# Injection and output matrices of the state space turned by VectorE in 32 by 32 blocks, placed by transfers; six parameter loads moved up

## The chip, the cores and the metric

The kernel runs on one core of a Trainium2 chip. The metric is the device time of one execution, in microseconds (us); the time of a kernel is the median of several executions. In the names of the profile PE is TensorE, DVE is VectorE, ACT is ScalarE, POOL is GpSimd and SP is SyncE, which here only starts transfers.

## The reference, cut to what matters

The block has one layer: a SwiGLU feed-forward (half weight), a mixer with attention beside a state space model, and a second feed-forward. Everything is float32, with 1024 rows of 1024 features. The change touches only the matrices of the state space part:

```python
x = x + 0.5 * swiglu(rms_norm(x, ff1_norm[l]), ff1_w_gate[l], ff1_w_up[l], ff1_w_down[l])
h = rms_norm(x, mix_norm[l])
proj = h @ w_in[l]                      # q, k, v, u
...
def s5_ssm_glu(u, a_re, a_im, b_re, b_im, c_re, c_im, d_skip, log_dt, w_glu, b_glu):
    uf = u.reshape(bsz, L, N_SSM_GROUPS, SSM_GROUP_CH)          # 32 groups of 16 channels
    lam = lax.complex(a_re, a_im)                               # [32, 64]
    dt = jnp.exp(log_dt)[:, None]
    lam_bar = jnp.exp(lam * dt)
    b = lax.complex(b_re, b_im)                                 # [32, 64, 16]
    b_bar = ((lam_bar - 1.0) / lam)[..., None] * b
    c = lax.complex(c_re, c_im)                                 # [32, 16, 64]
    bu = jnp.einsum('blgh,gph->blgp', uf.astype(jnp.complex64), b_bar)
    ...                                                         # s[t] = lam_bar * s[t-1] + bu[t]
    y = jnp.real(jnp.einsum('blgp,ghp->blgh', states, c))
```

## The kernel before, in words

**Products.** Every large product is made in float32 precision from three TensorE matmuls of 128x512, on operands that are split into a high and a low part (`_hi`, `_lo`; lines 1168 to 1170). ScalarE makes the high parts, VectorE the low ones.

**First feed-forward.** Its up and gate products are 22 *instances* (`N_INST`), each made of seven block products; product (n, j) is the j-th of instance n. One block product is 12 matmuls. SP loads the weights of an instance in pairs (`load_pair`, L847 to L869, several instances before their use), ScalarE (`instance`, L1886) makes the high halves of weights, evacuates the PSUM banks (L1832) and VectorE (`instance`, L2646) makes sums, low halves and the activations. Results go to DRAM (`store_b`, `store_open`, `store_t`, L871 to L881). The down pass is 77 *steps* (7 products of 11 steps); each step needs one 256 KB `d_in` tile, loaded by `load_step` (L883 to L895) when the step `N_SLOT` = 6 places earlier is done, split by ScalarE (L1879) and VectorE (L2573). Weights `dw_*` and the residual `x` come in between, in a list written out in the SP function `ffn_loads`.

**Mixer.** After the down pass TensorE makes the columns of `proj` in the order `IN_ORDER`; the state space steps stand between them as `WITH_PE` says (a dictionary from a unit of `w_in` and half to a list): E transposes (`transposes_e`, L1481 to L1490), K products, I injections (`inject`, L1492 to L1503), Y outputs, v windows. `WITH_ACT` does the same for ScalarE. The order of the transfers is written out by hand on SP (L1083 to L1120). `store_u`, `load_u8` and `load_csn` take u through DRAM into eight-step form and bring rotation tables.

**State space.** Sequences are cut in chunks of T = 8 steps. Four kinds of matrices are needed: E (injection of u into the state at a chunk's end, 16 blocks j of 128 x 2 x 128), CL (output from the state), K (within a chunk) and rotation tables `cs`. GpSimd makes them during the first feed-forward: six small loads of `a_re`, `a_im`, `log_dt` (`small_loads`, L3082), loads of b and c, then the powers of lambda, `CT`-based output blocks, and last a loop of four rounds (`Fori`, L3328 to L3378), each of which makes four blocks j of E in `EBb`, stores them, waits for the store, makes the rotation table in the same tile and stores that:

```python
            pool.dma_start(eb_d[:, :, bass.ds(i * 4, 4), :], EBb[:, :, :, :]).then_inc(eb_stored, 16)
            pool.wait_ge(eb_stored, i * 32 + 32)
```

E comes back from DRAM in one 2 MB load (L1090) into `ebs`, with the state index on the partitions; TensorE turns it with 32 transposes of 128x128, eight calls of `transposes_e`, and ScalarE copies them into `Et` (`e_out`). The same holds for C: 4 GpSimd loads into `c_in`, 8 transposes on TensorE (`c_tiles`, before instance 10), four copies on ScalarE (`c_out`) into `CT`. VectorE's share of the parameters (`prepare`, L2706) stands before its instance 7.

Of the kernel before, what the change touches and what calls it, by code (L numbers as in the profile page):

```python
# [20 lines left out]
F32 = mybir.dt.float32  # L21
# [6 lines left out]
P = 128  # L28
# [81 lines left out]
def steps(text):  # L110
# [12 lines left out]
WITH_PE = {(1, 1): steps("m1"), (4, 0): steps("E0 E1 E2 E3"), (5, 0): steps("E4 E5 E6 E7"), (6, 0): steps("K0"), (6, 1): steps("I0"),  # L123
# [4 lines left out]
WITH_ACT = {3: steps("e0 e1 e2 e3 W3"), 4: steps("e4 e5 e6 e7 W4"), 5: steps("k0 k1 W5"), 6: steps("k2 k3"),  # L128
# [18 lines left out]

ROUND = [((kind, 2 * b + i) if kind == "K" else (kind, b), 0 if kind == "K" else i)
         for kind, b in sum((WITH_PE[o] for o in sorted(WITH_PE)), []) if kind in "KEIYv"
         for i in range(1 if kind in "Ev" else 2)]  # L150
# [266 lines left out]
def block_kernel(nc, x, ff1_norm, ff1_w_gate, ff1_w_up, ff1_w_down, mix_norm, w_in, sink, a_re, a_im,  # L417
# [85 lines left out]
    ebs = at("ebs", 64 * KB, [P, 2, NJ, P])  # L503
# [63 lines left out]
    bc_tmp = at("bc_tmp", a_v + 8 * KB, [P, 2, NJ, GH])  # L567
# [74 lines left out]
    eb_d = nc.dram_tensor("eb_scratch", (P, 2, NJ, P), F32, kind="Internal").ap()  # L642
# [72 lines left out]
    ct_ready = sem("ct_ready")  # L715
# [6 lines left out]
    pool_chain = sem("pool_chain")  # L722
    eb_stored = sem("eb_stored")
    cl_stored = [sem(f"cl_stored{i}") for i in range(2)]
# [8 lines left out]
    eb_loaded = sem("eb_loaded")  # L733
# [4 lines left out]
    e_ready = sem("e_ready")  # L738
    e_taken = sem("e_taken")
# [94 lines left out]
    def _(sp):  # L834
# [82 lines left out]

        def store_x(w, h):
            sp.dma_start(xs_d[:, :, hs(h)], xT[:, :, hs(h)]).then_inc(x_stored, 16)

        def ffn_loads(w, ends):
# [24 lines left out]
            store_b(w, N_PAIR - 1)  # L946

# [9 lines left out]
            for q in range(N_SLOT, N_DSTEP):  # L957
# [7 lines left out]
                if q in quarters:  # L965
                    load_x_back(*quarters[q])
                if q == 8:
# [73 lines left out]
        def load_csn(b):  # L1041
            sp.wait_ge(e_ready, 4 if b == 0 else 8)
# [46 lines left out]
        sp.wait_ge(eb_stored, 4 * 32 + 16)  # L1089
        sp.dma_start(ebs[:, :, :, :], eb_d).then_inc(eb_loaded, 16)  # L1090
# [74 lines left out]
    def _(pe):  # L1165
# [198 lines left out]
        def c_tiles():  # L1364

            pe.wait_ge(c_loaded, 64)
            for ri in range(2):
                for i in range(4):
                    last = nc.tensor.transpose(bank[6 + ri][:, i * P:(i + 1) * P],
                                               c_in[:, ri, i, :, :].rearrange("p a s -> p (a s)"), ident[:, :])  # L1370
                last.then_inc(ct_ready, 1)

# [52 lines left out]
        for n in range(2, N_INST):  # L1425
            if n == 10:
                c_tiles()
# [3 lines left out]
        def round_free(kind, b, i=0):  # L1431
# [13 lines left out]
            elif kind == "E":  # L1445
                pe.wait_ge(e_taken, b + 1)
# [34 lines left out]
        def transposes_e(b):  # L1481

            pe.wait_ge(eb_loaded, 16)
            round_free("E", b)
            for jj in range(2):
                for ri in range(2):
# [2003 lines left out]
```

## Time and profile before

| | us |
|---|---|
| median of 3 runs | 1592.4 (1592.19 to 1592.65) |
| span of the profiled execution | 1590.5 |
| TensorE busy in it | 1582.6 |
| VectorE, ScalarE, GpSimd busy | 1097.5, 715.6, 507.7 |
| DMA traffic | 229.01 MB, mean 144 GB/s |

The profiled execution's own span, 1590.5 us, is 1.9 us under the median of the timed runs; a time worked out from trace rows has to be raised by that to stand beside the median. TensorE was granted its full clock in all 40 slices of the page (2.4 GHz, of its two levels). The profile lists instructions with the line of the kernel that issued them. A row of a timeline gives start, duration, engine, line, operation, output<-inputs, shape, count, and in brackets the idle time before it with what ended it. For SP and for GpSimd's transfers it shows the time of the issue, not of the transfer; the views of transfers give the time from issue to landing.

### The profile page before, as it was taken

What the parts mean: (1) busy time and instruction counts of PE and PEld (TensorE: products, weight loads), DVE (VectorE), ACT (ScalarE), POOL (GpSimd) and SP (SyncE); (2) the same over time, 40 slices, a digit from 0 to 9 for tenths busy, and PEclk for the clock granted to TensorE, in tenths of its full rate; (3) what the DMA queues carried; (4) which work ended last, traced back from release to release, by engine and by line L of the source; (5) the groups of instructions that cost most, each with busy time, mean ns of one, the idle gap of its engine ahead of it and who ended that gap; (6) DMA issues with size and microseconds to landing.
All of it is one profiled execution on the core that took longest, in us unless ns stands there. A gap on an engine that the chain in (4) does not pass through costs nothing.

```text
span 1590.5 us, 22050 instructions
## 1 busy us (share of the span) xinstructions
PE 1582.6 (100%) x7553; PEld 1308.0 (82%) x7553; DVE 1097.5 (69%) x1733; ACT 715.6 (45%) x1325; POOL 507.7 (32%) x938
## 2 busy tenths in 40 slices
PE   9999999999999999999999999999999999999998
PEld 7888888888888888888887888888888888888887
DVE  7966667766678886854369768766566656578766
ACT  7544343443334445532557544434344343344444
POOL 3005788877767877323030250000000000000000
PEclk9999999999999999999999999999999999999999
DMA  8254334433488455766431141433333333885443
GB/s 285 94 80 112 118 124 146 147 135 121 167 325 260 135 139 136 268 188 147 104 133 41 51 137 53 131 108 106 106 106 107 106 106 127 310 278 152 123 110 139
DMA packets 150007, 229.01 MB, mean 144 GB/s; under 512 B 17416, under 2 KB 86672, under 8 KB 146320
## 3 DMA queue, kind: packets, MB, share of 16 engines
q1 hardware_dynamic: 146672, 219.97, 42.9%
q0 software_dynamic: 3072, 7.62, 2.5%
q8 instruction: 61, 1.00, 0.3%
q14 instruction: 42, 0.34, 0.1%
q10 hardware_dynamic: 160, 0.07, 0.0%
HBM read 153.47 MB, written 74.15 MB: 143 GB/s over the span
## 4 chain that ended last, share of the span: by engine, by line
PE 98%; POOL 1%; issue 0%; ACT 0%; DVE 0%; DMA 0%; DVEq 0%; POOLq 0%; ACTq 0%
PE bank L1168 31%; PE bank L1170 31%; PE bank L1169 31%; POOL ssq L3069 1%; PE bank L1548 1%; PE bank L1360 1%; PE bank L1575 1%; PE bank L1530 0%; PE bank L1501 0%; PE bank L1475 0%; PE bank L1561 0%; PE bank L1523 0%; PE bank L1709 0%; PE bank L1202 0%; PE bank L1395 0%
## 5 line engine op out<-in xcount | busy, mean ns | idle before, releaser
L1168 PE MATMUL bank<-hbhi,ws_lo 128*128 128x512 f32 x1040 | 405.2, 390 | 0.0
L1170 PE MATMUL bank<-hbhi,ws_hi 128*128 128x512 f32 x1040 | 404.7, 389 | 0.0
L1169 PE MATMUL bank<-hblo,ws_hi 128*128 128x512 f32 x1040 | 404.6, 389 | 0.0
L1170 PEld LDWEIGHTS bank<-hbhi,ws_hi 128*128 128x128 f32 x1040 | 195.3, 188 | 40.6
L1169 PEld LDWEIGHTS bank<-hblo,ws_hi 128*128 128x128 f32 x1040 | 195.3, 188 | 40.4
L1168 PEld LDWEIGHTS bank<-hbhi,ws_lo 128*128 128x128 f32 x1040 | 195.3, 188 | 40.4 <-issue 0.4
L1168 PE MATMUL bank<-d_hi,ws_lo 128*128 128x512 f32 x572 | 222.7, 389 | 0.0
L1170 PE MATMUL bank<-d_hi,ws_hi 128*128 128x512 f32 x572 | 222.5, 389 | 0.0
L1169 PE MATMUL bank<-d_lo,ws_hi 128*128 128x512 f32 x572 | 222.5, 389 | 0.0
L3069 POOL TENSOR_TENSOR ssq<-ssq,sqt 128x512 f32<-128x512 f32 x18 | 25.2, 1401 | 615.2 <-ACT sqt L1762 613.4
L1832 ACT ACTIVATE loc<-bank 128x512 f32<-128x512 f32 x160 | 95.6, 597 | 251.4 <-PE bank L1170 251.4
L1879 ACT ACTIVATE d_hi<-d_in 128x512 fp32r<-128x512 f32 x154 | 96.1, 629 | 201.1 <-DMA d_in<-b_scratch 200.7
L2403 DVE TENSOR_TENSOR ws_lo<-w_sum,ws_hi 128x512 fp32r<-128x512 f32 x160 | 114.7, 717 | 96.2 <-ACT ws_hi L1795 96.2
L2573 DVE TENSOR_TENSOR d_lo<-d_in,d_hi 128x512 fp32r<-128x512 f32 x154 | 112.4, 732 | 82.1 <-ACT d_hi L1879 81.9
L1795 ACT ACTIVATE ws_hi<-w_sum 128x512 fp32r<-128x512 f32 x160 | 100.2, 626 | 76.1 <-PE bank L1170 60.1
L1168 PEld LDWEIGHTS bank<-d_hi,ws_lo 128*128 128x128 f32 x572 | 107.4, 188 | 22.4
L1169 PEld LDWEIGHTS bank<-d_lo,ws_hi 128*128 128x128 f32 x572 | 107.4, 188 | 22.2
L1170 PEld LDWEIGHTS bank<-d_hi,ws_hi 128*128 128x128 f32 x572 | 107.4, 188 | 22.1
L1168 PE MATMUL bank<-hT_hi,w_lo 128*128 128x512 f32 x288 | 116.1, 403 | 0.0
L1169 PE MATMUL bank<-hT_lo,w_hi 128*128 128x512 f32 x288 | 112.4, 390 | 0.0
L1170 PE MATMUL bank<-hT_hi,w_hi 128*128 128x512 f32 x288 | 112.4, 390 | 0.0
L2403 DVE TENSOR_TENSOR ws_lo<-raw2a,ws_hi 128x512 fp32r<-128x512 f32 x78 | 55.4, 717 | 63.6 <-ACT ws_hi L1795 62.7
(322 smaller groups left out, 2700.0 us busy)
## 6 DMA issues: line engine op xcount, KB each, us to landing
b_scratch<-loc SPq DMA_DIRECT2D x42, 1024.0 KB, 7.3
d_in<-b_scratch SPq DMA_DIRECT2D x154, 256.0 KB, 3.2
raw2a<-in_ff_w_up_dram SPq DMA_DIRECT2D x42, 512.0 KB, 4.9
loc<-in_ff_w_gate_dram SPq DMA_DIRECT2D x36, 512.0 KB, 5.0
xT<-x_scratch SPq DMA_DIRECT2D x12, 1024.0 KB, 7.1
x_scratch<-xT SPq DMA_DIRECT2D x5, 2048.0 KB, 8.2
dw_lo_place<-in_ff_w_down_dram SPq DMA_DIRECT2D x8, 1024.0 KB, 7.6
x_in<-in_x_dram SPq DMA_DIRECT2D x8, 512.0 KB, 7.7
```

Source lines behind the costliest of these rows:

```text
L1168: nc.tensor.matmul(o, wl, rh, start=first, stop=False, skip_group_check=chain)
L1169: nc.tensor.matmul(o, wh, rl, start=False, stop=False, skip_group_check=chain)
L1170: return nc.tensor.matmul(o, wh, rh, start=False, stop=last, skip_group_check=chain)
L1360: last = nc.tensor.transpose(bank[X_BANK[2 * t + kh]][:, kk * P:(kk + 1) * P], x_in[t // 4][:, t % 4, k * P:(k + 1) * P], ident[:, :])
L1548: last = nc.tensor.matmul(o, qT[r, n, 2 * a:2 * a + 2, :].rearrange("p g q -> p (g q)"), kTp[r, n * CHUNK:n * CHUNK + P], start=True, stop ...
L1575: last = nc.tensor.matmul(bank[V_BANK[m]][kv * HD:(kv + 1) * HD, nn * 256:(nn + 1) * 256], vwin[:, 2 * m + nn, kv * HD:(kv + 1) * HD], pts ...
L1795: act.activation(as_block(ws_hi[b][:, :]), weights(n, s), ACT.Copy).then_inc(ws_hi_done, 1)
L1832: act.activation(snap[w][:, i, :], bank[inst_bank(n, role)][:, :], ACT.Copy).then_inc(snap_taken, 1)
L1879: act.activation(d_hi[q % N_SLOT][:, :], d_in[q % N_SLOT][:, :], ACT.Copy).then_inc(d_hi_done, 1)
L2403: dve.tensor_tensor(as_block(ws_lo[b][:, :]), weights(n, s), as_block(ws_hi[b][:, :].bitcast(F32)), ALU.subtract).then_inc(ws_lo_done, 1)
L2573: dve.tensor_tensor(d_lo[q % N_SLOT][:, :], d_in[q % N_SLOT][:, :], d_hi[q % N_SLOT][:, :].bitcast(F32), ALU.subtract).then_inc(d_lo_done, 1)
L3069: pool.tensor_tensor(ssq_of(norm, h), ssq_of(norm, h), sqt_of(norm, a), ALU.add).then_inc(ssq_done, 1)
```

## The change

- **E.** After each round's four blocks GpSimd signals `eb_made` and waits for `eb_turned` instead of for a store. VectorE turns the blocks with two block transposes, each of which transposes every 32x32 square of a 128x512 tile within its own place (`turn_e`: `EBb` to `EBt`), before its instances 15 and 20 and at the down steps 20 and 52. SP moves the squares to their places with 16 transfers per round of 32 partitions x 8 x 32 elements each (`store_et` to `et_scratch`, 256 pieces of 128 bytes a transfer): after the load of pair 18, after the last `store_b` ahead of the down pass, and at down steps 28 and 60. In the mixer SP loads the result straight into `Et` in two halves of 1 MB; the second waits for the last `hT_lo`. `load_csn(0)` and `load_csn(1)` now stand before it, the two others one place earlier than they did. `ebs`, the TensorE transposes and the ScalarE copies are gone.
- **C.** 16 SP transfers (after the load of pair 3) of 16 partitions each, then two block transposes on VectorE (`turn_c`, before instance 6) into `CT`. `prepare` goes from before instance 7 to before instance 5.
- **Parameters.** The six small loads wait for products (2,0) to (2,5) instead of (2,0), (2,3), (3,0), (3,3), (4,0) and (4,3).
- A few scratch tiles get places of their own.

The diff, cut; lines with only "..." stand for what is left out:

```diff
-WITH_PE = {(1, 1): steps("m1"), (4, 0): steps("E0 E1 E2 E3"), (5, 0): steps("E4 E5 E6 E7"), (6, 0): steps("K0"), (6, 1): steps("I0"),
+WITH_PE = {(1, 1): steps("m1"), (6, 0): steps("K0"), (6, 1): steps("I0"),
...
-WITH_ACT = {3: steps("e0 e1 e2 e3 W3"), 4: steps("e4 e5 e6 e7 W4"), 5: steps("k0 k1 W5"), 6: steps("k2 k3"),
+WITH_ACT = {3: steps("W3"), 4: steps("W4"), 5: steps("k0 k1 W5"), 6: steps("k2 k3"),
...
+E_TURN_INST = {15: 0, 20: 1}
+E_TURN_STEP = {20: 2, 52: 3}
+E_STORES = 4 * 4
...
-    c_in = at("c_in", a_v + 2 * KB, [P, 2, 4, 2, NS])
+    c_in = at("c_in", a_v + 2 * KB, [P, 2, 8, 32])
...
+    EBt = at("EBt", a_v + 6 * KB, [P, 4, 2, P])
+    ptmp_e = at("ptmp_e", a_v + 10 * KB, [P, 2, 256])
...
+        def store_et(i):
+
+            sp.wait_ge(eb_turned, 2 * i + 2)
+            for a in range(P // 32):
+                for b in range(P // 32):
+                    sp.dma_start(et_d[32 * b:32 * b + 32, 4 * i:4 * i + 4, :, 32 * a:32 * a + 32].rearrange("c j r s -> c (j r) s"),
+                                 EBt[32 * a:32 * a + 32, :, :, 32 * b:32 * b + 32].rearrange("c j r s -> c (j r) s")
+                                 ).then_inc(et_stored, 16)
+
+        def load_c():
+
+            for n, c in enumerate((c_re, c_im)):
+                for g2 in range(2):
+                    for sh in range(2):
+                        for jj in range(2):
+                            q = 64 * g2 + 32 * sh + GH * jj
+                            sp.dma_start(c_in[q:q + GH, n, :, :],
+                                         c[0].rearrange("(j a g) h s -> a g h j s", a=2, g=2)[jj, g2][:, :, 32 * sh:32 * sh + 32]
+                                         ).then_inc(c_loaded, 16)
...
                 load_pair(N_INST * w + j)
+                if (w, j) == (0, 3):
+                    load_c()
+                elif (w, j) == (0, 18):
+                    store_et(0)
...
             store_b(w, N_PAIR - 1)
+            if w == 0:
+                store_et(1)
...
+                if w == 0 and q in (28, 60):
+                    store_et(2 + (q == 60))
...
         load_in(2)
         sp.wait_ge(down_out, 28)
-        sp.wait_ge(eb_stored, 4 * 32 + 16)
-        sp.dma_start(ebs[:, :, :, :], eb_d).then_inc(eb_loaded, 16)
+        sp.wait_ge(et_stored, 4 * E_STORES * 16)
+        sp.wait_ge(eb_stored, 4 * 16 + 16)
+        sp.dma_start(Et[:, 0:8, :, :], et_d[:, 0:8, :, :]).then_inc(et_loaded, 16)
...
         load_in(3)
         sp.wait_ge(down_taken, 32)
         sp.dma_start(xs_d[:, 0:4, hs(1)], xT[:, 0:4, hs(1)]).then_inc(x_parked, 16)
+        load_csn(0)
+        load_csn(1)
+        wait_lo(sp, 2 * KD)
+        sp.wait_ge(et_loaded, 16)
+        sp.dma_start(Et[:, 8:16, :, :], et_d[:, 8:16, :, :]).then_inc(et_loaded, 16)
         load_in(4)
         store_u(0)
-        load_csn(0)
         load_u8(0)
         load_in(5)
         store_u(1)
-        load_csn(1)
+        load_csn(2)
         load_u8(1)
         store_u(2)
-        load_csn(2)
+        load_csn(3)
         load_u8(2)
-        load_csn(3)
...
         for n in range(2, N_INST):
-            if n == 10:
-                c_tiles()
             instance(n)
...
-        def transposes_e(b):
-
-            pe.wait_ge(eb_loaded, 16)
-            round_free("E", b)
-            for jj in range(2):
-                for ri in range(2):
-                    m = 2 * jj + ri
-                    last = nc.tensor.transpose(bank[round_bank("E", b)][:, m * P:(m + 1) * P],
-                                               ebs[:, ri, 2 * b + jj, :], ident[:, :])
-            last.then_inc(e_ready, 1)
-
         def inject(b):
 
-            pe.wait_ge(e_taken, 2 * b + 2)
+            pe.wait_ge(et_loaded, 16 * (b // 2 + 1))
             pe.wait_ge(u8_loaded, 16 * T * (b + 1))
...
+                if q in E_TURN_STEP and w == 0:
+                    turn_e(E_TURN_STEP[q])
...
+        def turn_e(b):
+
+            dve.wait_ge(eb_made, b + 1)
+            if b:
+                dve.wait_ge(et_stored, 16 * E_STORES * b)
+            for ri in range(2):
+                dve.transpose(EBt[:, :, ri, :], EBb[:, ri, :, :]).then_inc(eb_turned, 1)
...
-                if n == 7:
+                if n == 5:
                     prepare()
+                elif n == 6:
+                    turn_c()
+                if n in E_TURN_INST and w == 0:
+                    turn_e(E_TURN_INST[n])
                 instance(n)
...
+        def turn_c():
+
+            dve.wait_ge(c_loaded, 16 * 16)
+            for ri in range(2):
+                dve.transpose(CT[:, ri, :, :].rearrange("p j h -> p (j h)"),
+                              c_in[:, ri, :, :].rearrange("p j s -> p (j s)")).then_inc(ct_taken, 1)
...
-                    pool.wait_ge(product_done, products(2 + n, 3 * g2))
+                    pool.wait_ge(product_done, products(2, 2 * n + g2))
...
-                pool.wait_ge(product_done, products(4, 3 * g2))
+                pool.wait_ge(product_done, products(2, 4 + g2))
...
-            passed()
-            pool.dma_start(eb_d[:, :, bass.ds(i * 4, 4), :], EBb[:, :, :, :]).then_inc(eb_stored, 16)
-            pool.wait_ge(eb_stored, i * 32 + 32)
+            passed().then_inc(eb_made, 1)
+            pool.wait_ge(eb_turned, i * 2 + 2)
```

## Rows read from the trace of the kernel before

**Rows 1.** The page's head and its part 1, busy us (share) xinstructions.

```profile
span 1590.5 us, 22050 instructions
...
PE 1582.6 (100%) x7553; PEld 1308.0 (82%) x7553; DVE 1097.5 (69%) x1733; ACT 715.6 (45%) x1325; POOL 507.7 (32%) x938
```

**Rows 2.** Waits of TensorE: us in total, times, longest; the longest of four.

```profile
PE bank L1407 <- POOL eps_t L3133: 1.4, 1, 1.4
```

**Rows 3.** Chain that ended last, 650 to 700 us: start, us, group.

```profile
677.12 1.75 PE bank L1488 x16
```

**Rows 4.** Timeline of VectorE, 460 to 474 us: the split of a down step.

```profile
469.03 0.75 DVE L2573 TENSOR_TENSOR d_lo<-d_in,d_hi 128x512 fp32r<-128x512 f32 x1 [2.30 <-ACT d_hi L1879]
```

**Rows 5.** Timeline of GpSimd, 60 to 131 us.

```profile
103.34 0.82 POOL L3105 DMA_DIRECT2D par<-in_log_dt_dram  x1 [10.06 <-PE bank L1170]
111.50 0.82 POOL L3105 DMA_DIRECT2D par<-in_log_dt_dram  x1 [7.34 <-PE bank L1170]
130.16 0.82 POOL L3111 DMA_DIRECT2D b_raw<-in_b_re_dram  x1 [17.84 <-DMA par<-in_log_dt_dram]
```

**Rows 6.** Transfers, 100 to 131 us: packets, MB, share; issues with us to landing.

```profile
q0 software_dynamic: 64, 0.01, 50.9%
...
b_scratch<-loc SPq DMA_DIRECT2D x2, 1024.0 KB, 14.6
loc<-in_ff_w_gate_dram SPq DMA_DIRECT2D x2, 512.0 KB, 4.9
raw2a<-in_ff_w_up_dram SPq DMA_DIRECT2D x2, 512.0 KB, 9.1
```

**Rows 7.** Tile `eb_scratch`: ns min/median/max, first and last start in us.

```profile
L3354 POOL DMA_DIRECT2D eb_scratch<-EBb x4: 667/679/682, 339.0 to 582.5; - x4
```

**Rows 8.** Timeline of SP, 68 to 125 us (issues).

```profile
68.37 0.93 SPq L868 DMA_DIRECT2D raw2a<-in_ff_w_up_dram  x2
73.18 0.92 SPq L868 DMA_DIRECT2D loc<-in_ff_w_gate_dram  x2
```

**Rows 9.** Timeline of SP, 654 to 704 us, in the mixer.

```profile
677.77 0.34 SPq L1029 DMA_DIRECT2D u_scratch<-ust  x1
...
681.38 3.83 SPq L1039 DMA_DIRECT2D u<-u_scratch  x8
...
691.23 4.40 SPq L1039 DMA_DIRECT2D u<-u_scratch  x8
```

**Rows 10.** Timeline of ScalarE, 84 to 92 us.

```profile
84.84 0.63 ACT L1795 ACTIVATE ws_hi<-loc 128x512 fp32r<-128x512 f32 x1
86.76 0.60 ACT L1832 ACTIVATE loc<-bank 128x512 f32<-128x512 f32 x1 [1.29 <-PE bank L1170]
```

**Rows 11.** Timeline of SP, 430 to 475 us, the opening of the down pass.

```profile
445.57 0.32 SPq L873 DMA_DIRECT2D b_scratch<-loc  x1
...
457.59 3.04 SPq L895 DMA_DIRECT2D d_in<-b_scratch  x2
...
471.19 3.04 SPq L895 DMA_DIRECT2D d_in<-b_scratch  x2
```

**Rows 12.** Two windows: length, busy us of each engine, clock, DMA share, GB/s.

```profile
446.00:454.00 8.00, 8.00 (x37) 6.60 (x36) 7.96 (x10) 1.78 (x3) 6.82 (x8) 1.00 0.91 312
454.00:462.00 8.00, 8.00 (x37) 6.64 (x36) 5.96 (x10) 2.24 (x4) 0.00 (x0) 1.00 0.97 356
```

**Rows 13.** Timeline of VectorE, 655 to 760 us: the last `hT_lo`.

```profile
675.02 0.69 DVE L2368 TENSOR_TENSOR hT_lo<-htmp,hT_hi 128x512 fp32r<-128x512 f32 x1 [0.70 <-ACT hT_hi L1778]
```

**Rows 14.** Tile `u` on SP, 690 to 697 us: issues, and time to landing.

```profile
L1039 SPq DMA_DIRECT2D u<-u_scratch x8: 321/431/1198, 691.2 to 694.4; - x8
...
DMA to landing us min/median/max: 2.3/2.4/3.1
```

**Rows 15.** Timeline of TensorE, 694 to 703 us: injection 1.

```profile
701.16 1.97 PE L1501 MATMUL bank<-u,Et 128*64 128x128 f32 x32
```

**Rows 16.** The page's part 6: issues, KB each, us to landing.

```profile
k_scratch<-zero POOLq DMA_DIRECT2D x4, 56.0 KB, 3.9
```

More of the change, by code:

```diff
@@ L145 @@
 STATE_STEPS = 4 * 5 + 8
+E_TURN_INST = {15: 0, 20: 1}
+E_TURN_STEP = {20: 2, 52: 3}
+E_STORES = 4 * 4
 ROUND = [((kind, 2 * b + i) if kind == "K" else (kind, b), 0 if kind == "K" else i)
-         for kind, b in sum((WITH_PE[o] for o in sorted(WITH_PE)), []) if kind in "KEIYv"
-         for i in range(1 if kind in "Ev" else 2)]
+         for kind, b in sum((WITH_PE[o] for o in sorted(WITH_PE)), []) if kind in "KIYv"
+         for i in range(1 if kind == "v" else 2)]
 def round_number(kind, b, i=0):
@@ L722, in block_kernel @@
     pool_chain = sem("pool_chain")
+    eb_made = sem("eb_made")
+    eb_turned = sem("eb_turned")
+    et_stored = sem("et_stored")
     eb_stored = sem("eb_stored")
+    et_loaded = sem("et_loaded")
     cl_stored = [sem(f"cl_stored{i}") for i in range(2)]
@@ L1362, in x_tiles @@
                     last.then_inc(xt_done, 1)
-        def c_tiles():
-            pe.wait_ge(c_loaded, 64)
-            for ri in range(2):
[L1368 to L1371, printed above, removed]
         def first_half(norm):
@@ L1961, in ffn @@
             for n in range(N_INST * w + 2, N_INST * (w + 1)):
-                if n == 10:
-                    c_out()
                 instance(n)
@@ L1990, in x_out @@
                                ).then_inc(xt_act, 1)
-        def c_out():
-            for ri in range(2):
-                act.wait_ge(ct_ready, ri + 1)
-                for g2 in range(2):
-                    r = slice(g2 * NS, (g2 + 1) * NS)
-                    src = bank[6 + ri][r, :].rearrange("p (j g h) -> p g j h", g=2, h=GH)[:, g2]
-                    act.activation(CT[r, ri, :, :], src, ACT.Copy).then_inc(ct_taken, 1)
         act.dma_start(ident[:, :], ident_c).then_inc(ident_loaded, 16)
@@ L2058, in _ @@
             norm_hi(N_MIX, i)
-        act.wait_ge(eb_stored, 4 * 32 + 16)
+        act.wait_ge(et_stored, 4 * E_STORES * 16)
+        act.wait_ge(eb_stored, 4 * 16 + 16)
         split_in(1)
@@ L2077, in k_out @@
             act.activation(dst, src, ACT.Copy).then_inc(k_act, 1)
-        def e_out(b):
-            act.wait_ge(e_ready, b + 1)
-            if b == 0:
-                wait_lo(act, 2 * KD)
-            act.activation(Et[:, 2 * b:2 * b + 2, :, :],
-                           bank[round_bank("E", b)][:, :].rearrange("p (j r m) -> p j r m", j=2, r=2), ACT.Copy
-                           ).then_inc(e_taken, 1)
         def y_out(b):
@@ L2150, in split_later @@
             split_hi(u, free)
-        step = {"k": k_out, "e": e_out, "y": y_out, "X": exponentials, "C": p_out, "O": o_out, "g": gelu,
+        step = {"k": k_out, "y": y_out, "X": exponentials, "C": p_out, "O": o_out, "g": gelu,
                 "s": square_att, "W": split_later, "q": lambda i: act.activation(mark[:, :], eps_t[:, :], ACT.Sqrt), "n": lambda h: norm_std(N_ATT, h),
@@ L3112, in load_b @@
                            (b_re, b_im)[n][0].rearrange("(j g) p h -> g p j h", g=2)[g2]).then_inc(b_loaded, 16)
-        def load_c(n, a):
-            pool.dma_start(c_in[:, n, :, a, :], (c_re, c_im)[n][0].rearrange("(i g) h p -> (g h) i p", g=8)
-                           ).then_inc(c_loaded, 16)
         def norm(which):
@@ L3249, in _ @@
         for k in range(1, T):
-            if k % 2:
-                load_c(k // 4, k // 2 % 2)
             tt(t0, lr[k], lr[1], ALU.mult)
@@ L3345, in _ @@
                 ilink(pool.tensor_copy(cR[:, ri], rot8[:, ri, bass.ds(i * 4, 4)]))
-            q = [ptmp[:, n, 0:4 * GH].rearrange("p (j h) -> p j h", h=GH) for n in range(2)]
+            q = [ptmp_e[:, n, 0:4 * GH].rearrange("p (j h) -> p j h", h=GH) for n in range(2)]
             for t in range(T):
@@ L3359, in _ @@
             while n < NC:
-                v = [ptmp[:, m, 0:4 * n].rearrange("p (j c) -> p j c", j=4) for m in range(2)]
+                v = [ptmp_e[:, m, 0:4 * n].rearrange("p (j c) -> p j c", j=4) for m in range(2)]
                 w = [cR[:, m, :].unsqueeze(2).to_broadcast([P, 4, n]) for m in range(2)]
```

25 lines of the change are left out of this document (8 added, 17 removed).

## The prediction, made before the changed kernel ran

> **What bounds the kernel.** I read the page first: TensorE has a matmul in flight for 1582.6 of 1590.5 us [rows 1]. Then its waits: four in the whole run, none longer than the first, 1.4 us at the start [rows 2]. So from the first products to the final norm TensorE's program order is the time: whatever leaves it is gained in full, unless something becomes late enough to stop it. After that I read, stage by stage, how late the inputs of the next matmul already are: the Sync (SP) queue, ScalarE and VectorE around the places where the change puts its transfers.
>
> **What leaves TensorE.** 32 transposes of `ebs` (L1488) in two runs of 16, and 8 of `c_in` (L1369). A run of 16 takes 1.75 us [rows 3], 0.109 us each, so 40 take 4.4 us. That is the whole possible gain: the eight `e_out` and four `c_out` copies of ScalarE end no wait of TensorE, and their removal costs and brings nothing.
>
> **What is added on VectorE.** Two block transposes for C and eight for E, 512 columns each. No row shows such an operation; the nearest from below is a 512-column subtraction, 0.75 us, and twice that bounds it above [rows 4]; I take 0.75. VectorE is idle 31% of the span [rows 1] and works an instance ahead, so 1.5 us at a time (at most 3) is covered by its waits. Its new wait is for GpSimd: block 0 is turned before instance 15. GpSimd's `log_dt` issues wait for products (4,0) and (4,3), 8.16 us apart [rows 5]: 2.72 us a product, 19.04 an instance of seven. Product (4,0) is done at 103.3, so instance 4 starts near 100.6 and instance 15 eleven instances later, at about 310 to 311. Behind that wait stand the weight parts of instance 16.
>
> **The six parameter loads and GpSimd.** They now follow products (2,0) to (2,5). Products (2,4) and (2,5) are 14 x 2.72 before (4,4) and (4,5), that is at 76.1 and 78.9; the two `log_dt` loads go out there instead of at 103.3 and 111.5 [rows 5]. In the old trace GpSimd then waits until 130.16, 18.6 us after the last issue. The software queue holds 50.9% of 16 engines over 31 us with 0.01 MB [rows 6]: 15.8 us on every engine for the two, 7.9 each. Back to back behind an issue at 76.1 they land at about 95 to 103. GpSimd starts 27 to 35 us earlier, its four `c_in` issues are gone, and block 0, stored at 339.0 [rows 7], is made at about 300 to 308, before VectorE asks. Afterwards GpSimd waits for VectorE, not for a store, and a block with its table takes it about 81 us ((582.5 - 339.0) / 3 [rows 7]), against turns at instance 20 (near 406), step 20 (498) and step 52 (585): 87 us apart or more, so each block is made 6 us or more before its turn, and the last table is out near 623, long before the mixer loads it. Cost: none; were the cover gone, VectorE would wait a few us, TensorE less.
>
> **The first thing that can be late: instance 4's weights.** SP issues instance 3's second pair at 68.37 and the first of instance 4's at 73.18 [rows 8]. Between them now stand 16 `load_c` issues. Eight such issues (16 partitions) take 3.83 us [rows 9], 0.47 each, so 16 take 7.5 and instance 4's pair goes out at 76.9, just as `log_dt` reaches the engines. What that means is in the window of the old `log_dt` loads: two stores of b beside them needed 14.6 us in the median and a pair of weights 9.1, where the pair ahead of them took 4.9 [rows 6]. ScalarE takes instance 4's first block at 84.84 and must then evacuate a bank at 86.76 [rows 10]; product (3,0) is done at 103.34 - 19.04 = 84.3, so the product that needs this bank starts two products later, at 89.7, so the pair must be in SBUF by 88.3. Free: 76.9 + 5.5 = 82.4, no stall. Behind one `log_dt` load: about 78 + 9 + 3.5 = 90.5, a stall of 2.2. Behind both: near 99, 11 us. Which queue comes first is decided by some tenths of a us. I take 2.0; ends 0 and 11. The Trainium skill ("DMA: Bandwidth & Descriptors", section "Queues, rings and completion order") has each engine go round its queues a packet at a time. By that rule the pair would get its turn between the two loads, so 2.2 and not 11; the landing times above agree as far as they go.
>
> **The second: the opening of the down pass.** After the last store of b (445.57 [rows 11]) SP issues 16 `store_et` transfers, 7.5 us, while `load_step(6)` was to go one us after that store. Their 256 pieces of 128 bytes are covered by the issue if a piece costs little. The DMA engines are 0.91 busy at 446 to 454 and 0.97 at 454 to 462, 312 and 356 GB/s [rows 12]. Of the 2.5 MB of the first window 1 MB is the store ahead; 1.5 MB is pushed behind the hold, and GpSimd's 0.5 MB table, now some 12 us earlier, leaves the second: 1.0 MB at 356 GB/s, so loads land about 2.8 us later. `d_in` for step 10, issued at 457.59 or later [rows 11], is split by VectorE at 469.03 to 469.78 [rows 4], and step 10 begins at 471.19, when the load of step 15 is released [rows 11]. Slack 1.4, stall 1.4; I take 1.5. Ends: 0 (other transfers give way) and 7.5 (the hold passed on whole). `store_et(0)` at 332, `store_et(2)` at 507 and `store_et(3)` at 594 hold SP for 7.5 us too; there a load is issued 13.6 us before its step and used to land in 3 to 6, so I cost them at nothing (if their cover were gone: up to 3 us each).
>
> **The third: u8 in the mixer.** SP's list after the down pass changes: the first half of E (1 MB for 2 MB) and CL, then `load_csn(0)`, `load_csn(1)`, a wait for the last hT_lo (its subtraction starts at 675.02 [rows 13]), the second half of E (1 MB), and only then `load_in(4)` (0.5 MB), which used to be over by then. `store_u(0)` at 677.77 finds 1.5 MB ahead of it in the queue; alone it landed in 3.6 us, at 681.38 when the u8 loads begin [rows 9]. At 356 GB/s 1.5 MB take 4.4 us, 1 of them over before 677.8, so it lands 2.3 to 3.4 later, and SP passes this on: `load_u8(1)` begins at 691.23 [rows 9], its last issue, at 694.4, lands within 3.1 us, at 697.5 [rows 14], so now at about 700.2. Injection 1 was at 701.16 [rows 15]; without 32 transposes it is at 697.7. Stall 2.5; ends 0 and 3.5. K, Y and later injections keep 3 us or more.
>
> **Sum.** 1590.5 - 4.4 + 2.0 + 1.5 + 2.5 = 1592.1. The median of the runs is 1.9 above this execution's span, so 1594.0, against 1592.4. A measurement of this kernel can tell about 0.2%, 3.2 us: 1589.2 to 1595.6 is "same".
>
> **Rivals.**
> **All of it is covered (B).** For it: every term above is a race decided by 1 to 3 us, and TensorE has no wait now [rows 2]. Against: three tight places would all have to be free. 1592.4 - 4.4 = 1588.0; with one small stall of 1 us, 1589.0.
> **Small writes are slow (C), the slower side.** At 446 to 454 4096 pieces of 128 bytes go to DRAM. For it: nothing in the old trace writes pieces under 448 bytes, and the smallest pieces it reads, 4 bytes of `log_dt`, cost 7.9 us per 64 on an engine, 0.12 each. At that price, the far end, `store_et` lasts 32 us. Against: 56 KB in 448-byte pieces landed in 3.9 us [rows 16], 128 pieces, no sign of a cliff there. It decides from 0.029 us a piece (7.5 us per 256 on an engine); at 0.05, 12.8 us, the loads of steps 6 to 10 slip by 5.3 more, 1.5 becomes 6.8, and `store_et(2)` may add 2: 1599.3 to 1601. The Trainium skill (same page, "Specifications") puts 512 bytes as the least size for full rate and has a read-modify-write below it; no row here shows a 128-byte write, and the sum above goes without it.
> **Both `log_dt` loads get ahead of instance 4's pair (D).** The same race lost twice: 11 for 2.0, 1603. Against: in the old window a store of b got through beside each of the two loads, late but not stopped for both [rows 6].
> That the transposes stay on TensorE cannot be: their functions are gone.
>
> **Chances.** My case A 0.52, with 1588.5 to 1598 as its own range (0.42 of it within 0.2%, 0.10 above); B 0.28; C 0.14; D 0.06. Faster by over 0.2%: 0.28; same 0.42; slower 0.10 + 0.14 + 0.06 = 0.30. The range runs from B at its best, 1587.8, to C's middle, 1600.5, and leaves out D and C's end.
>
> **What would show it.** Right: TensorE's waits list ScalarE's bank copy or `ws` near 90 us, `d_lo` near 470, and an injection waiting for `u` near 698; GpSimd's `b_raw` load at 95 to 105; VectorE's first `EBt` at 311 to 313 with no wait for GpSimd. Wrong: no wait of TensorE between 15 and 900 us (then B); `d_in` landings over 15 us after 446 (then C); instance 4's pair landing after 95 (then D); or VectorE waiting for `EBb` at instance 15 or 20, which I cost at nothing.

## The result, and the profile after

The changed kernel takes 1614.99 us (1613.5 to 1615.99, 4 runs), the kernel before 1592.53 us beside it: a ratio of 1.014, 95% interval 1.0129 to 1.0152. It is 22.5 us slower; 1594.0 was forecast, with 1600.5 as the upper end.

The head and part 1 of the page of the changed kernel, which answer to [rows 1]:

```profile
span 1612.6 us, 22030 instructions
...
PE 1584.5 (98%) x7513; PEld 1306.6 (81%) x7513; DVE 1103.0 (68%) x1743; ACT 709.8 (44%) x1313; POOL 491.9 (31%) x930
```

TensorE has 40 instructions fewer and stands still for 28 us instead of 8. Its list of waits (us in total, times, longest us), which answers to [rows 2], says where:

```profile
PE bank L1205 <- ACT loc L1845: 13.7, 1, 13.7
PE bank L1205 <- DVE d_lo L2568: 4.7, 3, 2.4
PE bank L1514 <- issue: 1.9, 1, 1.9
PE bank L1435 <- POOL eps_t L3144: 1.4, 1, 1.4
```

The first three are the places that the prediction named: instance 4's weights (place 1, at 89 us), the opening of the down pass (place 2, 475 to 489), and injection 1 (place 3). Together they are 20.3 us. The rest shows in these windows (from and to; length, TensorE busy, granted clock, DMA share, GB/s; no other engine is listed):

```profile
100.00:104.00 4.00, 1.15 (x3) 0.50 0.60 182
104.00:108.00 4.00, 4.00 (x12) 0.55 0.01 2
108.00:112.00 4.00, 4.00 (x20) 1.00 0.00 0
```
```profile
489.00:494.00 5.00, 5.00 (x17) 0.66 1.02 410
718.00:726.00 8.00, 6.11 (x55) 0.79 0.67 212
```

After each of the three places TensorE runs for some us at the lower of its two levels (1.2 instead of 2.4 GHz). In the chain that ended last a matmul then takes 0.43 us for 0.23:

```profile
107.03 0.43 PE bank L1205
107.46 0.36 PE bank L1206
107.82 0.23 PE bank L1207
```

What that costs is the length of the stretch times (1 - clock). From the restart at 102.9 on it is 1.1 x 0.50 + 4 x 0.45 = 2.4 us at place 1; 5 x 0.34 = 1.7 at place 2; 8 x 0.21 = 1.7 at place 3, of which some 1.5 is time in which it worked. The account, by spans of the two profiled executions: -4.1 (the transposes of C 0.8, of E 3.3, from the times of the same matmul either side of the transposes) + 13.7 + 2.4 + 4.7 + 1.7 + 1.9 + 1.5 = 21.8, against 22.1 measured; the rest is in gaps too short for the list.

**Place 1.** Timelines of SP and of GpSimd, then the landing times of tile `loc` from 70 to 104 us:

```profile
68.09 0.93 SPq L874 DMA_DIRECT2D raw2a<-in_ff_w_up_dram  x2
69.06 3.85 SPq L940 DMA_DIRECT2D c_in<-in_c_re_dram  x8
72.95 4.54 SPq L940 DMA_DIRECT2D c_in<-in_c_im_dram  x8
77.53 0.98 SPq L874 DMA_DIRECT2D loc<-in_ff_w_gate_dram  x2
```
```profile
75.86 0.81 POOL L3121 DMA_DIRECT2D par<-in_log_dt_dram  x1 [1.91 <-PE bank L1207]
78.58 0.82 POOL L3121 DMA_DIRECT2D par<-in_log_dt_dram  x1 [1.91 <-PE bank L1207]
```
```profile
DMA to landing us min/median/max: 13.5/18.6/23.6
```

Instance 4's weights come in two transfers, the first issued at 77.53 (73.18 in [rows 8]). The first lands at 91.0 (77.53 + 13.5), the second at 101.6, and the kernel waits for both. ScalarE, which copies a bank only after the piece of weights ahead of it in its order ([rows 10]), stands from 84.7 to 101.6. What all DMA engines moved from 66 to 103 us, in 40 slices of 0.93 us:

```profile
GB/s 4 0 0 12 256 378 384 212 45 55 36 18 19 1 2 1 0 0 0 23 46 65 93 123 245 258 202 61 0 0 0 8 49 79 113 97 182 221 244 143
```

There is little from 74 to 84 (C's small pieces to 78, then the first `log_dt` load), a burst of up to 258 GB/s near 90, nothing for nearly 3 us, and the rest only from 95 on, behind the second.

**Place 2.** SP, then all engines by window as in [rows 12]:

```profile
461.63 0.32 SPq L879 DMA_DIRECT2D b_scratch<-loc  x1
462.00 9.23 SPq L929 DMA_DIRECT2D et_scratch<-EBt  x16
471.33 0.40 SPq L901 DMA_DIRECT2D d_in<-b_scratch  x1
```
```profile
462.00:470.00 8.00, 8.00 (x37) 6.64 (x36) 5.31 (x9) 0.40 (x1) 6.37 (x15) 1.00 0.66 179
470.00:478.00 8.00, 5.63 (x26) 4.38 (x25) 1.21 (x2) 1.15 (x2) 6.51 (x20) 1.00 0.78 187
478.00:486.00 8.00, 7.61 (x34) 5.99 (x33) 5.86 (x9) 2.19 (x4) 6.97 (x14) 1.00 1.04 404
486.00:494.00 8.00, 6.10 (x21) 4.58 (x20) 4.04 (x6) 3.34 (x6) 3.01 (x8) 0.79 1.04 405
```

Where the kernel before moved 312 and 356 GB/s ([rows 12], the same work 16 us earlier), this one moves 179 and 187 while SP is busy with small transfers and just after them, and has to make it up at over 400 in the 16 us after that. The DMA engines are busy for only 0.66 and 0.78 of the two slow windows. TensorE waits for `d_lo` for 2.4 us until 477.6, then for 0.4 and 1.9 us, the last until 488.6.

**What costs nothing in this execution.** The block transposes and the landing of E's small writes are short (rows of tile `EBt`, ns min/median/max; of tile `et_scratch`, where 6.1 is one of the two loads of 1 MB back from it; of tile `CT`):

```profile
L2695 DVE STREAM_TRANSPOSE EBt<-EBb x8: 668/686/706, 328.8 to 609.1; 128x512 f32<-128x512 f32 x8
```
```profile
DMA to landing us min/median/max: 1.6/1.7/6.1
```
```profile
L2719 DVE STREAM_TRANSPOSE CT<-c_in x2: 398/414/431, 155.7 to 156.1; 128x256 f32<-128x256 f32 x2
```

VectorE does not wait for GpSimd at the turns here; GpSimd waits for it, 81.4 us in four times. That is not so in all the kernels below (see a3, best5 and best7).

### The profile page after: what moved, and what is told of

It reads as the page before. It is cut to its first block, busy times and chain, and to the rows that moved or that the text cites. A ratio compares the mean times of both kernels' runs of the same rounds, so it can differ in the third digit from the quotient of the medians.

```text
span 1612.6 us, 22030 instructions
## 1 busy us (share of the span) xinstructions
PE 1584.5 (98%) x7513; PEld 1306.6 (81%) x7513; DVE 1103.0 (68%) x1743; ACT 709.8 (44%) x1313; POOL 491.9 (31%) x930
## 4 chain that ended last, share of the span: by engine, by line
PE 95%; DMA 3%; DVE 1%; SPq 1%; ACT 1%; issue 1%; DVEq 0%; ACTq 0%
PE bank L1205 30%; PE bank L1206 30%; PE bank L1207 30%; DMA loc<-in_ff_w_gate_dram 1%; DMA d_in<-b_scratch 1%; PE bank L1514 1%; PE bank L1561 1%; PE bank L1588 0%; PE bank L1543 0%; SPq L940 0%; PE bank L1499 0%; PE bank L1574 0%; PE bank L1536 0%; DMA x_in<-in_x_dram 0%; PE bank L1722 0%
## 5 line engine op out<-in xcount | busy, mean ns | idle before, releaser
L1205 PE MATMUL bank<-hbhi,ws_lo 128*128 128x512 f32 x1040 | 406.2, 391 | 13.7 <-ACT loc L1845 13.7
L1206 PEld LDWEIGHTS bank<-d_lo,ws_hi 128*128 128x128 f32 x572 | 107.8, 188 | 22.1
```

The source lines that it names most:

```text
L1205: nc.tensor.matmul(o, wl, rh, start=first, stop=False, skip_group_check=chain)
L1206: nc.tensor.matmul(o, wh, rl, start=False, stop=False, skip_group_check=chain)
```

## The experiments

Each kernel is the changed one with the edit shown, unless said otherwise. Times are medians; the kernel before took 1592.3 to 1592.4 beside all of them.

### a1: C behind instance 4's weights

```diff
-                if (w, j) == (0, 3):
+                if (w, j) == (0, 4):
                     load_c()
```

> The 16 loads of C are issued after the weights of instance 4 instead of before them; nothing else differs from the changed kernel. Theory Q (a lost race of queues): the weights of instance 4, held 4.4 us by the loads of C (issued at 77.53 instead of 73.18), fell behind both log_dt loads. Then the 13.7 us wait of TensorE at 89 us is gone with the half clock after it, some 16 us in all: about 1599 us. Rival P (the parameter loads do it alone, wherever C is loaded): the wait stays, 1615. Rival S (the small pieces of C clog the queue for what comes behind them): the wait moves on to instance 5 or 6 and stays above 5 us, 1605 or more.

1601.1 us (1598.6 to 1602.7), 13.9 less. The 13.7 us wait and its half clock are gone; `loc` lands in 4.5 to 7.8 us and no wait takes its place in instances 5 or 6, although SP is held to 88.3 by the loads of C behind the full queue. In the profiled execution the matmul that stood at 108 us stands 16.0 us earlier. Some 1.7 of it is lost again later, most of it at injection 1, where the wait is 3.7 us for 1.9 and the half clock lasts longer. Q holds; P and S fall.

### a2: the kernel before with the parameter loads moved up

```diff
-                    pool.wait_ge(product_done, products(2 + n, 3 * g2))
+                    pool.wait_ge(product_done, products(2, 2 * n + g2))
...
-                pool.wait_ge(product_done, products(4, 3 * g2))
+                pool.wait_ge(product_done, products(2, 4 + g2))
```

> The kernel before with one thing of the change: the six parameter loads wait for products (2,0) to (2,5). Theory Q: instance 4's weights are issued at 73.2 and are in before log_dt reaches the engines at 77.6; no new wait of TensorE, 1592.5 within 1 us. Rival P: log_dt at 77.6 to 100 hinders instance 4 or 5 by itself: a wait of 5 us or more, 1598 to 1608.

1592.28 us against 1592.27, ratio 1.0 (0.999 to 1.001). The loads of `log_dt` go out at 76.2 and 78.9, but the weights are issued at 73.25:

```profile
73.25 0.93 SPq L868 DMA_DIRECT2D loc<-in_ff_w_gate_dram  x2
```

P falls: the move alone is free. It costs only together with the 4.4 us by which SP is held.

### a3: log_dt in rows of 128 bytes

```diff
+    dt_raw = at("dt_raw", a_v + 10 * KB + 2688, [P, NG])
...
-            for g2 in range(2):
-                pool.wait_ge(product_done, products(2, 4 + g2))
-                pool.dma_start(par[g2 * NS:(g2 + 1) * NS, 2, :],
-                               log_dt[0].rearrange("(j g) -> g j", g=2)[g2].partition_broadcast(NS)
-                               ).then_inc(params_loaded, 16)
+            pool.wait_ge(product_done, products(2, 4))
+            pool.dma_start(dt_raw[:, :], log_dt[0].partition_broadcast(P)).then_inc(params_loaded, 16)
...
+        for g2 in range(2):
+            link(pool.tensor_copy(par[g2 * NS:(g2 + 1) * NS, 2, :],
+                                  dt_raw[g2 * NS:(g2 + 1) * NS, :].rearrange("p (j g) -> p g j", g=2)[:, g2]))
```

> The changed kernel, with log_dt loaded as 128 rows of 128 bytes in one transfer and put in its places by two GpSimd copies, instead of two transfers of 1024 pieces of 4 bytes; the loads of C stay ahead of instance 4's weights. Theory Q: the hold of SP alone (issue at 77.5, 5 us to land) is harmless, the wait at 89 us is gone: about 1599 us, and the weights land by 84. Rival S (C's pieces or the hold itself make the wait): 5 us or more of the wait stay, 1604 or more.

1597.6 us (1596.9 to 1599.9), 17.4 less. The order of issues and the hold are the same (77.81), but the weights land in time:

```profile
77.81 0.98 SPq L875 DMA_DIRECT2D loc<-in_ff_w_gate_dram  x2
```
```profile
DMA to landing us min/median/max: 4.1/5.1/7.4
```

And `log_dt` itself, in the view of transfers from 66 to 103 us, takes 3.2 us; the two of the changed kernel take 18.3 in the median:

```profile
dt_raw<-in_log_dt_dram POOLq DMA_DIRECT2D x1, 16.0 KB, 3.2
```

So place 1 needs two things at once, the hold of SP and the `log_dt` loads in 4-byte pieces; either taken away ends it. The injection's wait is 3.5 us here, and there is a new one of 1.2 us near 640 us for a sum that GpSimd makes (`dw_hi_place`): its last round of E was late, and VectorE waited 5.5 us for it at step 52.

### c1: 12 of the 16 loads of C ahead of the weights

```diff
...
-                    load_c()
+                    load_c([(0, 0), (0, 1), (1, 0)])
+                elif (w, j) == (0, 4):
+                    load_c([(1, 1)])
...
```

> The changed kernel with 12 of the 16 loads of C ahead of instance 4's weights and 4 behind them, so that the weights are issued at about 75.3 instead of 77.5 (73.2 before). Theory Q: their transfers reach the engines some 1.5 us before log_dt does; a part gets through, and the last to land, behind one log_dt load, gives a wait of 0 to 4 us at 89 us: 1599 to 1604. If the wait is all or nothing with an edge nearer to 73, it stays at 12 or more and the time at 1613 to 1616.

1605.4 us, one run, just above the range of theory Q; the weights go out at 76.45 (not 75.3: the last four issues ahead of them took 2.87 us, 0.72 each), land within 4.0 and 14.1 us, at 80.5 and 91.1, and the wait at 89 us is 2.7, as theory Q has it. What the time has above the range fits the wait at injection 1, 3.5 us and its half clock for 1.9. The wait at 89 us:

```profile
PE bank L1207 <- ACT loc L1847: 2.7, 1, 2.7
```

In the changed kernel the weights go out 1.1 us later (1.6 later counted from the first `log_dt` issue, 75.86 there and 76.38 here), and TensorE waits 11 us longer. By these two executions the edge lies between 76.5 and 77.5; its price is a second `log_dt` load.

### b1: the second part of E ahead of the down pass

```diff
+                elif (w, j) == (0, 21):
+                    store_et(1)
...
             store_b(w, N_PAIR - 1)
-            if w == 0:
-                store_et(1)
```

> The changed kernel with the 16 transfers of the second part of E issued after the weights of instance 21, some 15 to 30 us before the down pass, instead of in its opening. Theory H (SP's hold of 9.2 us there pushes 2.5 MB of loads back): the waits for d_lo between 474 and 489 us and the half clock after them, 6.9 us in all, go: about 1608 us. Rival T (the opening is short of bandwidth because GpSimd's table and the other traffic came to lie there): at least 3 of the 6.9 us stay, 1611 or more.

1608.8 us, 6.2 less. No wait for `d_lo` is in the list, and the same two windows now move what they moved in the kernel before:

```profile
462.00:470.00 8.00, 8.00 (x37) 6.63 (x36) 7.36 (x12) 1.78 (x3) 6.65 (x13) 1.00 0.89 306
470.00:478.00 8.00, 8.00 (x37) 6.61 (x36) 5.66 (x8) 2.20 (x4) 6.90 (x15) 1.00 0.96 369
```

H holds and T falls: with the transfers out of the opening nothing is short there. The edit takes SP's hold and the small pieces away together; that it was the hold is read from the DMA share of 0.66 in the slow window, which left the engines a third of their time.

The wait at injection 1 is 4.0 here. Five kernels have the same order in the mixer: the changed one waits 1.9 in its profiled execution, a1 3.7, a3 3.5, b1 4.0 and c1 3.5. Why it differs is open.

### b2 and b3: the order in the mixer

This is b2. In b3 `load_in(4)` alone moves ahead of `load_csn(0)`.

```diff
+        load_in(4)
         load_csn(0)
-        load_csn(1)
         wait_lo(sp, 2 * KD)
-        sp.wait_ge(et_loaded, 16)
-        sp.dma_start(Et[:, 8:16, :, :], et_d[:, 8:16, :, :]).then_inc(et_loaded, 16)
-        load_in(4)
         store_u(0)
+        load_csn(1)
...
         load_u8(1)
+        sp.wait_ge(et_loaded, 16)
+        sp.dma_start(Et[:, 8:16, :, :], et_d[:, 8:16, :, :]).then_inc(et_loaded, 16)
         store_u(2)
```

> The changed kernel with SP's order in the mixer mended: the fifth load of w_in and one table go before the wait for hT_lo, u's first store follows that wait at once, and the second half of E is loaded after the second group of u8. Theory U (in this execution of the changed kernel 1.5 MB or more queued ahead of store_u(0) made u8(1) late for injection 1): the 1.9 us wait at the injections and the half clock after it, 3.3 us in all, go; store_u(0) to the first u8 load back near 3.6 us from 6.9; about 1611.5 us. Rival V (injection 1 is short by itself once the 32 transposes are gone, whatever the order): a wait of 1 us or more stays, 1613 or more.

> The changed kernel with the fifth load of w_in alone moved ahead of the two tables; the second half of E (1 MB) stays ahead of store_u(0). Theory U: 0.5 MB less in the queue, some 1.4 us less between store_u(0) and the first u8 load (about 5.5 us), and a wait of 0.5 to 2.5 us stays at the injections: about 1613 to 1615. Rival V: as long as in the changed kernel, 1.9 to 4.

b2: 1612.95 us (1611.3 to 1615.0), 2.0 less, not clear of the changed kernel's 1613.5 to 1616.0. From `store_u(0)` to the first u8 load it is 3.0 us, and injection 1 waits no more: rival V, by which it waits whatever the order, falls. But theory U's time of 1611.5 is missed too, since a wait of 2.0 us is at injection 2 instead, ahead of whose `store_u(2)` the 1 MB of E now stands. So the waiting is as long as it was (2.0 for 1.9); what the profiled execution gained is the stretch at half clock, which did not follow this wait.

b3: 1615.7 us, one run, above theory U's range. The wait is 2.8 us, within rival V's band, and `store_u(0)`, issued at 700.87, is followed by u8 only at 708.54, 7.7 us for 6.9. The 0.5 MB of w_in were not what mattered. Since waits of 1.9 to 4.0 us are seen with the changed kernel's order, this one run does not decide between U and V. What still stands ahead of `store_u(0)` is `load_csn(1)`, which waits for `load_csn(0)` to land (11.0 us behind 1 MB of x and 2.3 MB of CL), and the half of E; which of the two it is was not tried apart.

### b4: the second half of E in two loads

```diff
+        load_in(4)
         load_csn(0)
-        load_csn(1)
         wait_lo(sp, 2 * KD)
+        store_u(0)
         sp.wait_ge(et_loaded, 16)
-        sp.dma_start(Et[:, 8:16, :, :], et_d[:, 8:16, :, :]).then_inc(et_loaded, 16)
-        load_in(4)
-        store_u(0)
+        sp.dma_start(Et[:, 8:12, :, :], et_d[:, 8:12, :, :]).then_inc(et_loaded, 16)
         load_u8(0)
...
+        load_u8(2)
+        sp.wait_ge(et_loaded, 32)
+        sp.dma_start(Et[:, 12:16, :, :], et_d[:, 12:16, :, :]).then_inc(et_loaded, 16)
...
-            pe.wait_ge(et_loaded, 16 * (b // 2 + 1))
+            pe.wait_ge(et_loaded, 16 * max(b, 1))
```

`load_csn(1)` to `load_csn(3)` stand after `store_u(1)`, `store_u(2)` and the last load of E.

> The changed kernel with the mixer's order mended another way: the second half of E in two loads of 0.5 MB, the one for injection 2 in the place that the first table had behind store_u(0), the one for injection 3 after the third group of u8, so that no load of 1 MB stands ahead of a store of u. Theory U: neither injection 1 nor injection 2 waits over 1 us; 3.3 us less than the changed kernel, 1611.5. Rival V: injection 1 or 2 is short by itself without the 32 transposes and waits 1 to 2.5 us, with the half clock after it: 1613 to 1615.

1612.1 us (1610.0 to 1612.6), 2.9 less. Neither injection 1 nor injection 2 waits, as theory U has it, but injection 3 does, 2.1 us, which the expectation had not named. Here too the waiting is no shorter: in the profiled execution neither the waits for `d_lo` (4.6 us in four) nor this one was followed by half clock, and that is the gain.

### best1 to best4: all three places mended

best1 is a1, b1 and b2 together; best2 is that with a3; best3 is a1, b1 and b4; best4 is best3 with another order on TensorE:

```diff
-           (7, 0): steps("I1 K1"), (7, 1): steps("I2"), (8, 0): steps("K2"),
+           (7, 0): steps("K1 I1"), (8, 0): steps("I2 K2"),
```

> All three mends together (C after instance 4's weights, the second part of E ahead of the down pass, the mixer's order): by theory no wait of TensorE over 1.5 us is left, and the 40 transposes are gained, 4.1 us by the two traces: 1588.4 us, range 1588 to 1590. Rival: a new wait takes a part of it (GpSimd, or the loads of steps 5 to 10): 1590 to 1593.

> As best1, and log_dt loaded in rows of 128 bytes with two GpSimd copies. By theory nothing waits for log_dt any more: 1588.4 us, the same as best1 within 0.5 us. Rival: GpSimd, some 20 us earlier, puts its stores and tables where they collide with the opening of the down pass: 1590 or more.

> C after instance 4's weights, the second part of E ahead of the down pass, and the mixer with E's second half in two loads: no wait of TensorE over 1.5 us left by theory U, 1588.4 us (1588 to 1589.5). By rival V a wait of 1 to 2 us at injection 1 or 2 and its half clock: 1590 to 1592.

> As best3, with injection 1 behind the second K product and injection 2 half a unit of w_in (2.7 us) later in TensorE's order. Here both theories give 1588.4 us (1588 to 1589.5), since the injections have the time back that the 32 transposes gave them; if it is 1 us or more under best3, rival V was right there.

1590.8 (ratio 0.9986 to 1.0004), 1591.8 (0.9987 to 1.0005), 1591.9 (0.9987 to 1.0007) and 1590.5 us (0.9982 to 1.0): none can be told from the kernel before by its interval, and all missed the 1588.4 us that theory gave them. Places 1 and 2 are gone from all; a wait at an injection is in each profile: 2.0 and 3.0 at injection 2 in best1 and best2, 2.4 and 2.1 at injection 3 in best3 and best4, where best4 also has 1.2 for a bank. best4 is 1.4 us under best3, which by its expectation speaks for rival V; but their intervals overlap, and in neither does injection 1 or 2 wait for u8, which is what V says. The wait left is at injection 3, which these expectations had not named.

best2's wait of 3.0 us, the longest of the four, was followed by full speed, best3's of 2.4 us by half clock: the same 32 matmuls of an injection take 1.97 us in one and 3.45 in the other. Injection 2 in best2, and the window with it (granted clock 1.00; only TensorE is listed):

```profile
708.52 1.97 PE L1515 MATMUL bank<-u,Et 128*64 128x128 f32 x32 [3.00 <-issue]
```
```profile
708.00:716.00 8.00, 7.48 (x79) 1.00 0.84 174
```

Injection 3 in best3, on TensorE, and its u8 loads on SP:

```profile
723.61 3.45 PE L1516 MATMUL bank<-u,Et 128*64 128x128 f32 x32 [2.43 <-issue]
```
```profile
713.08 0.43 SPq L1063 DMA_DIRECT2D u_scratch<-ust  x1
...
716.73 3.64 SPq L1073 DMA_DIRECT2D u<-u_scratch  x8
```

### best5 to best7: the chain of injection 3

best5 puts injection 3 later on TensorE; best6 puts its transfers earlier on SP; best7 has both. All on best3.

```diff
-           ... (8, 1): steps("K3"), (9, 1): steps("I3"),
-           (10, 0): steps("Y0"),
+           ... (8, 1): steps("K3"), (10, 0): steps("I3 Y0"),
```
```diff
         load_in(6)
+        store_u(3)
         load_m(0)
         store_k(1)
-        store_u(3)
+        load_u8(3)
         load_in(7)
-        load_u8(3)
```

> As best3 (all three mends; its profile has one wait, 2.4 us at injection 3, and 1.5 us of half clock in it), with injection 3 half a unit of w_in (2.7 us) later in TensorE's order. If what is left is the race of u8(3) with injection 3, which comes 3.5 us earlier without the 32 transposes, the wait is gone: 1588.4 us (1588 to 1589.5) and no wait over 1.5 us. Rival: something else is short by 2 us there (the second K round, Y0), and a wait of 1 to 2.5 us takes its place: 1590 to 1592.

> As best3, with TensorE's order kept and SP's changed: store_u(3) ahead of load_m(0), and load_u8(3) ahead of load_in(7), so that u8(3) is issued some 1.6 us earlier (716.7 in best3) and lands near 721, as injection 3 comes up. By the same theory the wait shrinks to 0 to 1 us: 1588.4 to 1590. Rival: load_m(0), 2 us later, makes Y0 wait instead: 1590 to 1592.

> Both mends of best5 and best6. By theory the 40 transposes are gained in full and with slack: 1588.4 us, spread of the runs as small as the kernel before's. Rival as in best6: Y0 waits for load_m(0), 1590 or more.

best6: 1588.29 us (1587.8 to 1588.8, 10 runs), ratio 0.9974, interval 0.9965 to 0.9984. best7: 1588.4 (0.997 to 0.9988), but with two of its 11 runs at 1592.0 and 1592.6, so its spread is not as small as expected. best5: 1589.3 (1587.8 to 1592.8; 0.9973 to 0.9991), whose profile, of a run of 1591.5, still has 0.6 us at injection 3, 1.1 for `d_lo` at 526, behind the third part of E (506.5 to 516.0 on SP), and 1.3 near 636 for GpSimd's sum `dw_hi_place`, which stands behind its last table (issued at 629.96; 623.37 in best6). best7 has 0.4 of the latter. No run tried to mend these two places. In best6, u8(3) is issued 1.9 us earlier and injection 3 starts as it comes up:

```profile
714.79 3.93 SPq L1073 DMA_DIRECT2D u<-u_scratch  x8
```
```profile
721.06 1.97 PE L1516 MATMUL bank<-u,Et 128*64 128x128 f32 x32
```

Its list of waits begins with the 1.4 us at the start that the kernel before had too, and nothing else in it is over 0.3:

```profile
PE bank L1437 <- POOL eps_t L3146: 1.4, 1, 1.4
PE bank L1207 <- DVE ws_lo L2400: 0.3, 1, 0.3
```

Y0 does not wait for `load_m(0)`. The transposes' 4.1 us are gained in full: 1592.33 - 1588.29 = 4.0. That the three places and the chain of injection 3 were all that stood in the way is shown by this kernel, not by adding up the single mends.

## Why the prediction was wrong

- **"40 take 4.4 us. That is the whole possible gain."** Right: 4.1 between the traces, 4.0 in best6.
- **VectorE and GpSimd.** Right for the changed kernel. A turn of 512 columns takes 0.686 us (0.75 taken); C's are of 256 columns, not 512, 0.41 us each. GpSimd's first b load is at 101.7 (forecast 95 to 105), the first turn at 328.8, 16 us after the forecast of 311 to 313, with the whole loss of place 1 in between, and it waits for nothing. But "each block is made 6 us or more before its turn" and "Cost: none" do not hold in a3, best5 and best7: VectorE waited 5.5, 5.9 and 4.7 us for the last block at step 52, and TensorE 1.2, 1.3 and 0.4 us for the sum that GpSimd makes next. The prediction looked for the mixer's load of the last table, not for that sum. Why GpSimd's last round was longer there is open.
- **Place 1, the step that failed: "I take 2.0; ends 0 and 11."** The mechanism (the weights come behind `log_dt`), the issue at 77.53 (76.9 forecast) and the price of one `log_dt` load were right. What failed is the choice between the outcomes: the pair counts as in when the second of its two transfers is. The first landed at 91.0, behind one `log_dt` load, where the prediction had the pair ("90.5"); the second landed at 101.6, behind both, and TensorE waited 13.7 us. That is rival D, by its own sign ("landing after 95"; "near 99", 11 us), which had a chance of 0.06 and lay outside the range. In c1, where the pair goes out 1 us earlier, its last transfer landed at 91.1 and the wait was 2.7. With the clock place 1 cost 16.1 us for 2.0, and that is 14.1 of the 20.5 us by which the forecast span was missed. The text itself had this race decided "by some tenths of a us", and then took the value by an argument for one queue's turn. The rule cited (each engine goes round its queues, "DMA: Bandwidth & Descriptors" in the Trainium skill, "Queues, rings and completion order") did not decide it: the first transfer got its turn between the two `log_dt` loads, as the rule has it, and the second still came behind both.
- **No term for the clock.** 2.4 + 1.7 + 1.5 = 5.6 us, a quarter of the loss, came after the waits, and the sum had nothing for it. The trace of before could not show it, since its longest wait was 1.4 us.
- **Place 2: "Slack 1.4, stall 1.4."** The place, the buffer (`d_in`) and the cause (H in b1) were right, the size not: 4.7 us in three waits and 1.7 of clock. The hold was 9.23 us, not 7.5, and what it took from the engines (312 to 179 GB/s) was more than could be made up in time. The end given was 7.5, so 6.4 lies within it, at 4.9 over the 1.5 taken.
- **Place 3: 2.5 us.** In the changed kernel 1.9 measured and 1.5 of clock, and `store_u(0)` needs 3.3 us more to land (2.3 to 3.4 forecast). The mechanism was right; the size was in part luck of this execution, since four other kernels with the same order waited 3.5 to 4.0, at or above the end of 3.5, and in a1 `store_u(0)` needed 8.8 us, 5.2 more than before.
- **"K, Y and later injections keep 3 us or more."** Wrong: in the kernel before, the last of u8(3) is issued by 720.6 and lands some 2.5 us later, 2.0 before injection 3 at 725.10. That is less than the 3.3 by which the injections moved up without E's transposes. In the changed kernel it does not show, since the delay at injection 1 gives that time back; b4, best3 and best6 show it.
- **Rival C (small writes)** falls: E's transfers of 256 pieces of 128 bytes landed 1.7 us after issue in the median, and no `d_in` landing of the opening took over 13.5 us (its sign was 15). The Trainium skill ("DMA: Bandwidth & Descriptors", "Specifications") has such pieces below full rate, and by the windows of place 2 they are: 179 GB/s at a DMA share of 0.66, where the kernel before moved 312 at 0.91. But the engines had time left, so it is SP's issue that sets the pace.

## What to carry to other kernels

Moving work from the engine that is the bound to the queues adds issues, and a queue issues in order: 16 small transfers held SP for 8.4 to 9.4 us, and what they cost is read from what stands behind them, not from their bytes. Where a race is decided within a microsecond, give both outcomes like odds, follow the last transfer that the consumer waits for and not the first, and keep loads in 4-byte pieces away from any load with a due time. Time taken off a busy engine is only gained down to the shortest slack of every chain that feeds it afterwards: list them all, the later ones too. A single mend can move a wait without shortening it, as b2 and b4 did.

## What was not expected of the hardware

- A short wait of TensorE may or may not be followed by a stretch at its 1.2 GHz level. In the changed kernel the waits of 13.7 us, of 1.9 us until 488.6 and of 1.9 us at injection 1 were; the wait of 2.4 us until 477.6 was not (granted clock 1.00 from 470 to 486), nor were waits of 2.0 us in b2 and best1, 2.1 in b4 and 3.0 in best2. After the 13.7 us wait it ran at half clock from the first matmul to 107.8; after the wait until 488.6 the clock fell only near 490, with TensorE at work again. So two executions with the same waits can differ by 1.5 us or more.
- Two transfers of 4 KB in 4-byte pieces kept others back for some 20 us (weights issued at 77.53 to 78.01 landed at 91.0 and 101.6); the same 32 numbers loaded for all 128 partitions in 128-byte rows landed in 3.2 us.
- The other mended kernels, best6 aside, scatter more than the kernel before, whose 26 runs beside best5 to best7 lie within 0.8 us but for two: best3 goes from 1589.1 to 1596.7. best6 stays within 1.0 us over 10 runs. best7 does not, although its profile, of a run at its median, has no wait over 0.4 us but the one at the start; what the longer runs waited for was not profiled.
